# Feature blocks of 128 in place of every eighth feature, and the third expert matrix issued from Pool

## The reference: what is computed

```
xf = rms_norm(h, ln_g)                            # 512 x 1024
... softmax over 4 groups, top 1; softmax over its 8 experts, top 2 ...
for each of 32 experts e, for the rows xb of xf routed to it:
    yb = (silu(xb @ w1[e]) * (xb @ w3[e])) @ w2[e]  # w1, w3: 1024 x 512, w2: 512 x 1024
y = sum of each token's two rows yb, weighted
```

## Time and profile before

| | us |
|---|---|
| three runs, median (lowest, highest) | 2631.13 (2630.28, 2631.23) |
| the profiled execution | 2635.05 |
| its span, first to last instruction | 2633.1 |
| PE busy | 2406.6 (91%) |
| DVE, ACT, POOL busy | 759.7, 486.8, 299.8 |
| MoE experts, layer 0 (first gather to last result) | 839.98 to 1472.80 |

### The profile page before, as it was taken

One profiled execution on the slowest core, in us unless ns is written; L12 is line 12 of the kernel. 1 busy time (PEld: TensorE's weight loads), 2 busy tenths in 40 slices (PEclk: granted clock), 3 DMA queues, 4 the chain that ended last, 5 costly groups with the idle time before them and its releaser, 6 DMA issues.

```text
span 2633.1 us, 30883 instructions
## 1 busy us (share of the span) xinstructions
PE 2406.6 (91%) x11934; PEld 1550.6 (59%) x11934; DVE 759.7 (29%) x1862; ACT 486.8 (18%) x1207; POOL 299.8 (11%) x569
## 2 busy tenths in 40 slices
PE   6999899999987999999999399999979999999993
PEld 2344689999936555655655146766455555555551
DVE  4208545555472210111010230466222101101102
ACT  2212244444411000000000111266110000000001
POOL 0000456666400000000000100011000000000001
PEclk9999599999997999999999699999979999999996
DMA  8121160000034677877887621100245778778773
GB/s 235 33 79 51 20 69 2 2 2 2 21 124 213 255 321 324 361 322 325 350 334 300 249 64 33 64 26 26 96 192 230 322 321 376 311 319 366 320 310 133
DMA packets 52631, 493.89 MB, mean 188 GB/s; under 512 B 6565, under 2 KB 11429, under 8 KB 35591
## 3 DMA queue, kind: packets, MB, share of 16 engines
q1 hardware_dynamic: 39942, 466.71, 45.3%
q10 hardware_dynamic: 10240, 16.79, 1.8%
q0 software_dynamic: 2304, 8.39, 1.0%
HBM read 458.38 MB, written 32.43 MB: 186 GB/s over the span
## 4 chain that ended last, share of the span: by engine, by line
PE 89%; DVE 4%; issue 2%; ACT 2%; DMA 2%; POOL 0%; ACTq 0%; DVEq 0%; POOLq 0%; PEldq 0%
PE bank L1256 85%; PE bank L1728 1%; DVE arena L1059 1%; PE bank L1457 1%; DMA arena<-y_rows,ints 1%; ACT arena L527 1%; PE bank L1533 1%; PE bank L1264 1%; DVE arena L1207 1%; DMA y_rows<-arena 0%; DVE arena L784 0%; POOL arena L501 0%; DMA arena<-x 0%; PE bank L1400 0%; ACT arena L757 0%
## 5 line engine op out<-in xcount | busy, mean ns | idle before, releaser
L1256 PE MATMUL bank<-arena 128*128 128x128 f32 (+7 forms) x10322 | 2218.4, 444 | 77.2 <-DVE arena L1059 44.5
L1256 PEld LDWEIGHTS bank<-arena 128*128 128x128 f32 (+2 forms) x10322 | 1388.2, 203 | 857.2 <-issue 755.3
L653 ACT ACTIVATE arena<-bank 128x512 f32<-128x512 f32 x64 | 38.2, 597 | 1072.2 <-PE bank L1256 1072.2
L625 ACT ACTIVATE arena<-bank 128x256 f32<-128x256 f32 (+3 forms) x512 | 176.2, 350 | 223.2 <-PE bank L1256 164.2
L997 DVE TENSOR_TENSOR arena<-bank,vec 128x512 f32<-128x512 f32 x64 | 44.3, 692 | 600.2 <-PE bank L1256 600.2
L501 POOL DMA_INDIRECT arena<-y_rows,ints x16 | 18.2, 1139 | 1508.4 <-DMA y_rows<-arena 1500.2
L430 POOL TENSOR_TENSOR arena<-arena,const 128x128 f32<-128x128 f32 x384 | 164.6, 458 | 115.3 <-PE bank L1256 92.8
L1051 DVE TENSOR_TENSOR arena<-arena,bank 128x256 f32<-128x256 f32 x64 | 26.9, 421 | 353.6 <-ACT arena L649 353.6
L1264 PE MATMUL bank<-const,arena 128*128 128x128 f32 x128 | 26.1, 367 | 69.3 <-DVE arena L784 69.2
L893 DVE TENSOR_TENSOR arena<-bank,arena 128x128 f32<-128x128 f32 x256 | 70.3, 292 | 59.1 <-PE bank L1256 59.0
L757 ACT ACTIVATE arena<-arena,small 128x128 f32<-128x128 f32 (+3 forms) x128 | 70.4, 552 | 25.1 <-DVE small L1207 25.1
(11 more groups left out here) (193 smaller groups left out, 1104.0 us busy)
## 6 DMA issues: line engine op xcount, KB each, us to landing
arena<-m_w SPq DMA_DIRECT2D x64, 4096.0 KB, 19.1
arena<-m_w SPq DMA_DIRECT2D x64, 2048.0 KB, 12.0
y_rows<-arena ACTq DMA_DIRECT2D x128, 128.0 KB, 8.8
y_rows<-arena SPq DMA_DIRECT2D x2, 3840.0 KB, 41.3
arena<-kv_w SPq DMA_DIRECT2D x3, 2048.0 KB, 14.9
rev_bias<-arena SPq DMA_DIRECT2D x1, 5120.0 KB, 54.2
arena<-a_wk SPq DMA_DIRECT2D x8, 512.0 KB, 9.4
arena<-a_wv SPq DMA_DIRECT2D x8, 512.0 KB, 3.6
```

Of the source, the lines that this page charges most:

```text
L625: nc.scalar.activation(dst(n), src, ACT.Copy).then_inc(sem("ev_" + name), 1)
L653: nc.scalar.activation(yb[:, n % 2, :], bank[6 + n % 2][:, :], ACT.Copy).then_inc(sem("yb_ready"), 1)
L1256: return nc.tensor.matmul(dst, lhsT, rhs, start=start, stop=stop)
```

## The change

On the chip, every strided group `k::NK` becomes a contiguous block `P * k : P * k + P`; the numbers of instructions and their shapes stay. The weights follow: a weight whose rows are read from DRAM by groups is now read in contiguous row blocks, and the others (the LoRA, router, key/value, query, gate and expert matrices and the gains) are laid out on the host so that each partition reads one contiguous run, as before. The expert weights keep their sizes and their layout of rows, `[partition, 3 x 4096]` per expert. Besides, the w2 load of every expert moves from `moe_loads` on SP to the head of `moe_pool` on Pool, with the same conditions; for expert 0 of layer 0, which on SP had none but its place behind the `a_wo` loads, it waits on `pe_s` and `ev_s`.

```diff
-                rows = d[w].rearrange("(p k) n -> k p n", k=NK)
+                rows = d[w].rearrange("(k p) n -> k p n", k=NK)
...
             def moe_loads(l):
                 for e in range(E):
                     n = E * l + e
-                    for i, (lo, hi) in enumerate(((0, 2 * U), (2 * U, 3 * U))):
-                        if l == 0 and e == 0:
-                            pass
-                        elif l == 0 and e == 1:
-                            sp.wait_ge(sem("y_ready"), NP)
-                        elif l == 0 and e == 2:
-                            sp.wait_ge(sem("wo_mm"), 8)
-                        elif l == 1 and e == 0:
-                            sp.wait_ge(sem("o_added"), at("o_added", ROUNDS))
-                        elif l == 1 and e < 3:
-                            sp.wait_ge(sem("h_nsa"), 8)
-                        else:
-                            sp.wait_ge(sem("hidden_mm" if i == 0 else "expert_mm"), n - 2)
-                        dst = w13_flat[n % 3] if i == 0 else w2_slot[n % 3]
-                        sp.dma_start(dst, d["m_w"][l, e, :, lo:hi]).then_inc(sem(f"w{i}_in{n % 3}"), 16)
+                    if l == 0 and e == 1:
+                        sp.wait_ge(sem("y_ready"), NP)
+                    elif l == 0 and e == 2:
+                        sp.wait_ge(sem("wo_mm"), 8)
+                    elif l == 1 and e == 0:
+                        sp.wait_ge(sem("o_added"), at("o_added", ROUNDS))
+                    elif l == 1 and e < 3:
+                        sp.wait_ge(sem("h_nsa"), 8)
+                    elif e >= 3:
+                        sp.wait_ge(sem("hidden_mm"), n - 2)
+                    sp.dma_start(w13_flat[n % 3], d["m_w"][l, e, :, 0:2 * U]).then_inc(sem(f"w0_in{n % 3}"), 16)
...
             def moe_pool(l):
+                for e in range(E):
+                    n = E * l + e
+                    if l == 0 and e == 0:
+                        pool.wait_ge(sem("pe_s"), PACKS)
+                        pool.wait_ge(sem("ev_s"), PACKS)
+                    elif l == 0 and e == 1:
+                        pool.wait_ge(sem("y_ready"), NP)
+                    elif l == 0 and e == 2:
+                        pool.wait_ge(sem("wo_mm"), 8)
+                    elif l == 1 and e == 0:
+                        pool.wait_ge(sem("o_added"), at("o_added", ROUNDS))
+                    elif l == 1 and e < 3:
+                        pool.wait_ge(sem("h_nsa"), 8)
+                    else:
+                        pool.wait_ge(sem("expert_mm"), n - 2)
+                    nc.gpsimd.dma_start(w2_slot[n % 3], d["m_w"][l, e, :, 2 * U:3 * U]).then_inc(sem(f"w1_in{n % 3}"), 16)
...
-                        last = nc.tensor.transpose(bank[k][:, P * j:P * j + P], xn[:, j, k::NK], ident)
+                        last = nc.tensor.transpose(bank[k][:, P * j:P * j + P], xn[:, j, P * k:P * k + P], ident)
...
-                            last = mm(bank[2 + q][:, P * k:P * k + P], h[:, j, 4 * q + k::NK], onehot[:, p % 2, j, :],
+                            last = mm(bank[2 + q][:, P * k:P * k + P], h[:, j, P * (4 * q + k):P * (4 * q + k) + P], onehot[:, p % 2, j, :],
                                       j == 0, j == NJ - 1)
...
-                                last = mm(bank[2][:, CAP * k:CAP * k + CAP], h[:, j, k::NK], onehot[:, 1, j, 0:CAP],
+                                last = mm(bank[2][:, CAP * k:CAP * k + CAP], h[:, j, P * k:P * k + P], onehot[:, 1, j, 0:CAP],
                                           j == 0, j == NJ - 1)
...
+    def by_rows(w):
+
+        return w.reshape(NK, P, -1).transpose(1, 0, 2).reshape(P, -1)
```

More of the change, by code:

```diff
@@ L291, in _ @@
             sp.dma_start(vec[:, :], d["vecs"]).then_inc(sem("vec_in"), 16)
-            sp.dma_start(w1l, d["a_w1"].rearrange("(p k) n -> p k n", k=NK)).then_inc(sem("lora1_in"), 16)
-            sp.dma_start(a1l, d["a_a1"].rearrange("(p k) n -> p k n", k=NK)).then_inc(sem("lora1_in"), 16)
-            sp.dma_start(g1l, d["a_g1"].rearrange("(p k) n -> p k n", k=NK)).then_inc(sem("lora1_in"), 16)
+            sp.dma_start(w1l, d["a_w1"].rearrange("p (k n) -> p k n", k=NK)).then_inc(sem("lora1_in"), 16)
+            sp.dma_start(a1l, d["a_a1"].rearrange("p (k n) -> p k n", k=NK)).then_inc(sem("lora1_in"), 16)
+            sp.dma_start(g1l, d["a_g1"].rearrange("p (k n) -> p k n", k=NK)).then_inc(sem("lora1_in"), 16)
             sp.dma_start(w2l[0:64, :], d["a_w2"]).then_inc(sem("lora2_in"), 16)
@@ L328, in _ @@
                 sp.dma_start(wring[:, q % 4, :], wo_rows[m, :, :]).then_inc(sem(f"wring{q % 4}"), 16)
-            sp.dma_start(router_w, d["router_w"].rearrange("l (p k) n -> p l k n", k=NK)).then_inc(sem("router_in"), 16)
+            sp.dma_start(router_w, d["router_w"].rearrange("p (l k n) -> p l k n", l=2, k=NK)).then_inc(sem("router_in"), 16)
             sp.dma_start(router_b, d["router_b"].rearrange("l p n -> p l n")).then_inc(sem("router_in"), 16)
@@ L1811 @@
     a = {k: np.asarray(v) for k, v in inputs.items()}
-    x = {k: a[k][0] for k in ("x", "a_wr", "a_wk", "a_wv", "a_wo", "a_w1", "a_w2", "a_a1", "a_a2", "a_g1", "a_g2")}
+    def by_rows(w):
+        return w.reshape(NK, P, -1).transpose(1, 0, 2).reshape(P, -1)
+    x = {k: a[k][0] for k in ("x", "a_wr", "a_wk", "a_wv", "a_wo", "a_w2", "a_a2", "a_g2")}
+    x |= {k: by_rows(a[k][0]) for k in ("a_w1", "a_a1", "a_g1")}
     x["cmp_k_w2x2"] = np.concatenate([a["cmp_k_w2"]] * 2, 1)
@@ L1817 @@
     x["b_wo"] = a["b_wo"][0].reshape(NH, HD, D)[by_pair].reshape(D, D)
-    x["w_q"] = a["b_wqg"][0][:, 0:D].reshape(D, NH, HD)[:, by_pair].reshape(P, NK * D)
-    x["w_gate"] = a["b_wqg"][0][:, D:].reshape(D, NH, 3)[:, by_pair].reshape(P, NK * 48)
+    x["w_q"] = by_rows(a["b_wqg"][0][:, 0:D].reshape(D, NH, HD)[:, by_pair])
+    x["w_gate"] = by_rows(a["b_wqg"][0][:, D:].reshape(D, NH, 3)[:, by_pair])
     parts_kv = a["kv_w"].reshape(D, 6, 256)
-    x["kv_w"] = np.stack([parts_kv[:, pair].reshape(P, U) for pair in ([0, 1], [2, 4], [3, 5])])
-    x["m_w"] = np.concatenate([a["m_w1"].reshape(2, E, P, U), a["m_w3"].reshape(2, E, P, U),
-                               a["m_w2"].reshape(2, E, 4, P, D).transpose(0, 1, 3, 2, 4).reshape(2, E, P, U)], 3)
+    x["kv_w"] = np.stack([by_rows(parts_kv[:, pair]) for pair in ([0, 1], [2, 4], [3, 5])])
+    x["m_w"] = np.concatenate([w.reshape(2, E, n, P, U // n).transpose(0, 1, 3, 2, 4).reshape(2, E, P, U)
+                               for w, n in ((a["m_w1"], NK), (a["m_w3"], NK), (a["m_w2"], 4))], 3)
     vectors = {"a_ln": a["a_ln"][0], "kv_ln": a["kv_ln"], "b_ln": a["b_ln"][0], "m_ln0": a["m_ln"][0],
@@ L1827 @@
                "lnx_w": a["a_lnx_w"], "lnx_b": a["a_lnx_b"]}
-    x["vecs"] = np.concatenate([vectors[n].reshape(P, 8) for n in VEC_P]
+    x["vecs"] = np.concatenate([vectors[n].reshape(8, P).T for n in VEC_P]
                                + [by_tile[n].reshape(8, P).T for n in VEC_M], 1)
@@ L1832 @@
         x[f"pe_{n}"] = a[f"cmp_pe_{n}"].reshape(NG, 16, P).transpose(2, 1, 0)
-    x["router_w"] = np.concatenate([a["m_wg"], a["m_we"]], 2)
+    x["router_w"] = np.concatenate([by_rows(w) for w in np.concatenate([a["m_wg"], a["m_we"]], 2)], 1)
     x["router_b"] = np.broadcast_to(np.concatenate([a["m_bg"], a["m_be"]], 1)[:, None, :], (2, P, 36))
```

## The result

The changed kernel takes 2368.53 us (median of 4 runs, 2365.91 to 2369.54), the kernel before 2630.7 us (4 runs). The ratio is 0.9003, 95% interval 0.8988 to 0.9019: 262 us less.

A forecast was written before the change was run, and what follows sets the result against it. PE, busy 91% of the span, was taken as the bound. From the profiled 2635.05 us, minus 254.5 for gather plus 10 for DMA waits gave 2390.55; the median, 3.9 lower, was forecast at 2387 us, range 2360 to 2480.

The forecast's parts named there:

- The bound and the gather: PE bounds the kernel; 2048 gather records in the MoE go from 0.238 to 0.112 us, saving 258.0 us.
- The first gathers at 1.2 GHz: First 3.8 us of each layer's gather run at 1.2 GHz and gain less: 3.5 us off the saving, net 254.5.
- Transposes, other weights, the w2 move: Packed transposes, contiguous loads of the other weights and w2 loads on Pool: each taken as 0 us.
- DMA waits: In the expert loops, faster gather makes PE wait for weights: 10 us added, bounds 0 and 28 for both layers.
- the slack: Time to spare between expert 6's w1 and w3 landing and its hidden: 19.7 us before, 11.6 after the pair shrinks.
- Two of its signs: Expected in the changed profile: layer 0's experts end at 1344 to 1350, a pair takes 30.8 to 31.5 us.
- No sustained rate fell to 376 GB/s: Rival in the MoE loops: DMA engines cannot hold 426 GB/s; at 376, 2467 us in all; chance 0.22.
- The stride was not innocent: Rival on the gather: stride costs nothing, records stay at 0.238 us, time within 0.2% of 2631; chance 0.05.
- Pool's queue lands a w2 load: Rival in the expert loops: w2 loads on Pool take 21.2 us each, giving 2678 us; chance 0.07, near or past limit.
- the nearest row: Pool's indirect gather, 512 KB in 5.3 us; four such pieces in sequence gave the rival's 21.2 us a w2 load.

## Why the prediction was right, and where its size was off

- **The bound and the gather: right.** Forecast 0.238 to 0.112 us a record, measured 0.112; a pair of 30.76 us, measured 30.72. The strides show the cause. The rule of the Trainium skill that the prediction set against this part (TensorE: Matmul & The Clock Gate, section LDWEIGHTS: the columns alone, 107 ns) does not hold here: 128 columns take 192 or 336 ns by their stride.
- **The first gathers at 1.2 GHz: right in size.** Together they gave 6.6 + 5.3 = 11.9 us; the sum had 2 x (64 x 0.126 - 1.8) = 12.5.
- **Transposes, other weights, the w2 move: right at 0**, by the gather-only stride, by stride 8 and by the blocks on SP alone.
- **DMA waits: the term was too large.** I took 10 us and it was 0. The failed step is "a pair holds the DMA engines for 0.81 x 38.8 = 31.4 us", read as a need of 31.4 us, 0.7 more than the pair has. After the change the same product is 1.01 x 30.7 = 31.0, and it fits into 30.7: the share sums the packets' times and can pass 1.00, so it is no clock. The bytes are the better measure, 13.1 MB at the 427 GB/s now seen in 30.7 us. No deficit eats the slack: it is 22 us at expert 6 in the changed kernel and 9 us in the old order on SP, with no wait on weights to the end in either. The prediction had 11.6 us for the old order and 4 to 13 more from the earlier issue on Pool, and both came out near that; the slack by itself would have covered its own deficit of 10.5 us, so 10 us was a choice between its bounds of 0 and 28. That PE and DMA would be about level was right, and closer than I could know: the ceiling of 430 GB/s gives 13.1 / 0.430 = 30.5 us a pair, 0.2 us below what PE needs.
- **The clock: a term was missing.** Six stretches of 3.4 us at 1.2 GHz in the loops are gone, 6 x 1.7 = 10.2 us. The sum took the clock as unchanged, and the reading "repeats every 38.82 us through both layers, 15 times in each" passed over them: three pairs of each layer take 40.5 us. That they go with the slow gather is shown by the other runs (six at stride 8, five with the stride in the gather alone, one at stride 4, none at 2, none with blocks on SP), but not why.
- **The ledger of the miss.** Forecast 244.5 us off the profiled execution, measured 266.7: 22.2 more, of which 10 is the DMA term, 10.2 the clock, 1.4 the last results at a better clock (6.36 and 6.38 against 6.07 and 5.29 us), and the rest small. The forecast of 2387 stands 18 us above the result, inside its range. Both missed terms erred the same way. Two of its signs missed on the same side: layer 0 ends at 1335.00, not 1344 to 1350 (4.4 us from the stages ahead, 5.1 from the clock), and a pair at 30.72 lies just under 30.8 to 31.5.
- **The rivals.** No sustained rate fell to 376 GB/s: it is 427 over 400 us of layer 0, and the slices of layer 1 read the same. The 358 GB/s that the Trainium skill (DMA: Bandwidth & Descriptors, section Where 436 GB/s comes from) has for the HBM side is below the 427 of the changed kernel's loops, and the measurement decides. The stride was not innocent. Pool's queue lands a w2 load of 2048 KB in 15.8 us (median) with the DMA engines full, and PE never waits for one: the nearest row (512 KB in 5.3 us) was the wrong one to scale.

## What to carry to other kernels

Look at the distance between starts and at the weight load's time, not at matmul busy time: two groups of the same shape at 0.238 and 0.112 us differ by something that the shape doesn't show, here the stride of the stationary operand. If a contracted axis may be split in any order, choose the order in which the on-chip read is contiguous (for these float32 matmuls every second float was nearly as good), and let the host reorder the weights. Before cutting the engine that sets the pace, work out the rate at which it will ask for data: here the cut ended 0.2 us a pair above the DMA ceiling, and the next cut of 161 us gave 18 to 27.

## What the runs showed of the hardware

- A matmul's float32 weight load of 128 columns takes 192 ns at stride 1, 196 at 2, 329 at 4 and 336 at 8 floats. A transpose's takes 141, 209, 212 and 193 ns, and the transposes at stride 8 keep a pace of 0.11 to 0.12 us.
- The 16 DMA engines held 427 GB/s for 400 us of the changed kernel, with the loads from two queues, and 426 in the same stretch with all loads on one (879.5 to 1278.9 in both), result stores included.
- With PE's work cut and the loads late, stores of 128 KB landed in 22.2 us with the loads on two queues, against 11.2 with one. In the changed kernel, with two load queues and the DMA share at 1.01 as well, it was 12.5 us.
- PE fell to 1.2 GHz for 3.4 us every four pairs (157 us) in much of the loops before, and at strides of 8, once at stride 4, and not in the loops of the changed kernel. What makes it fall there is left open; DMA traffic is higher after the change, and PE's busy share about the same (29.32 of 30.70 us, against 37.39 of 38.80).
